# Down products of a split-precision FFN: eight PSUM banks in rotation instead of four

## What is computed

```python
def swiglu_ffn(x, g, w_gate, w_up, w_down):
    h = rmsnorm(x, g)
    return (jax.nn.silu(h @ w_gate) * (h @ w_up)) @ w_down

x = x + 0.5 * swiglu_ffn(x, ffn1_norm, ffn1_w_gate, ffn1_w_up, ffn1_w_down)
...                                    # mixers, cross attention
x = x + 0.5 * swiglu_ffn(x, ffn2_norm, ffn2_w_gate, ffn2_w_up, ffn2_w_down)
```

## Time and profile before

| | |
|---|---|
| runs shown | 3314.75, 3319.26, 3321.52 us; median 3319.26 |
| profiled execution, its own time | 3310.65 us |
| its span in the trace | 3308.9 us |
| TensorE matmul busy | 3157.0 us, 95% |
| VectorE busy | 1591.4 us, 48% |
| ScalarE busy | 925.1 us, 28% |
| GpSimd busy | 1164.7 us, 35% |
| mean granted TensorE clock | 0.991 of full speed |
| down phases of the 20 later turns: TensorE waits for `x_early`, `x_late` | 13.4 and 12.6 us |

### The profile page before, as it was taken

The page is one execution under the profiler, slowest core; times in us unless marked ns, Lnnn a source line. Parts: engine busy times, 40 slices in busy tenths (PEclk is TensorE's granted clock), DMA queues, the critical chain, the costliest instruction groups (busy, mean ns, idle before and its releaser), DMA issues.

```text
span 3308.9 us, 52314 instructions
## 1 busy us (share of the span) xinstructions
PE 3157.0 (95%) x19481; PEld 2993.7 (90%) x19481; DVE 1591.4 (48%) x2641; ACT 925.1 (28%) x1726; POOL 1164.7 (35%) x756
## 2 busy tenths in 40 slices
PE   6999999999999999999999999999899999999998
PEld 5999999999979888888887989988799999999997
DVE  3554445544546655653342456242328444455445
ACT  5222222212323333433423342132312222221123
POOL 3455555544422222211112034222124545444452
PEclk9999999999999999999999999999999999999999
DMA  5311111111143133211112145024301111111112
GB/s 186 134 39 39 51 38 57 45 38 38 66 149 130 56 130 124 82 62 49 65 43 75 49 160 177 28 91 168 132 32 39 39 45 44 38 58 43 38 38 77
DMA packets 92182, 247.52 MB, mean 75 GB/s; under 512 B 11536, under 2 KB 49168, under 8 KB 89360
## 3 DMA queue, kind: packets, MB, share of 16 engines
q1 hardware_dynamic: 48640, 154.09, 13.9%
q10 hardware_dynamic: 43408, 91.55, 7.7%
HBM read 197.87 MB, written 47.75 MB: 74 GB/s over the span
## 4 chain that ended last, share of the span: by engine, by line
PE 83%; DVE 9%; issue 3%; ACT 2%; POOL 1%; ACTq 1%; DVEq 0%; POOLq 0%
PE psum L168 55%; PE psum L264 13%; PE psum L2197 1%; DVE n_tmp L954 1%; PE psum L2133 1%; PE psum L1339 1%; PE psum L3167 1%; DVE f_h_hi L801 1%; PE psum L1409 1%; DVE f_hid L802 1%; PE psum L1384 1%; POOL w_lo L2672 1%; PE psum L3140 1%; DVE a_sc L1734 1%; PE psum L2147 1%
## 5 line engine op out<-in xcount | busy, mean ns | idle before, releaser
L133 POOL TENSOR_TENSOR w_hi<-w_raw,zero 128x1024 fp32r<-128x1024 f32 x79 | 158.9, 2012 | 1138.6 <-PE psum L264 788.7
L457 POOL TENSOR_TENSOR w_lo<-w_raw,w_hi 128x512 fp32r<-128x512 f32 x320 | 418.6, 1327 | 389.0 <-ACT w_hi L655 389.0
L168 PE MATMUL psum<-x_hi,w_hi 128*128 128x384 f32 x2288 | 463.8, 336 | 14.6 <-issue 4.6
L168 PE MATMUL psum<-x_lo,w_hi 128*128 128x384 f32 x2288 | 462.7, 336 | 0.0
L168 PE MATMUL psum<-x_hi,w_lo 128*128 128x384 f32 x2288 | 458.9, 334 | 0.0
L168 PEld LDWEIGHTS psum<-x_hi,w_hi 128*128 128x128 f32 x2288 | 402.1, 188 | 22.5 <-issue 13.2
L168 PEld LDWEIGHTS psum<-x_lo,w_hi 128*128 128x128 f32 x2288 | 404.2, 188 | 2.2 <-issue 0.6
L168 PEld LDWEIGHTS psum<-x_hi,w_lo 128*128 128x128 f32 x2288 | 402.2, 188 | 0.0
L168 PE MATMUL psum<-f_h_hi,w_hi 128*128 128x384 f32 x1056 | 271.8, 338 | 27.4 <-DVE x_early L760 13.4
L655 ACT ACTIVATE w_hi<-w_raw 128x512 fp32r<-128x512 f32 x320 | 192.6, 626 | 375.1 <-PE psum L168 312.2
L168 PE MATMUL psum<-f_h_hi,w_lo 128*128 128x384 f32 x1056 | 268.1, 334 | 0.0
(11 more groups left out here) (339 smaller groups left out, 4779.1 us busy)
## 6 DMA issues: line engine op xcount, KB each, us to landing
w_raw<-units SPq DMA_DIRECT2D x224, 512.0 KB, 3.8
gate_dram<-b_stash ACTq DMA_DIRECT2D x48, 192.0 KB, 1.9
e_gate<-gate_dram ACTq DMA_DIRECT2D x48, 192.0 KB, 2.7
a_kc<-k_cache ACTq DMA_DIRECT2D x4, 2048.0 KB, 8.5
a_vc<-v_cache ACTq DMA_DIRECT2D x4, 2048.0 KB, 13.0
proj_dram<-a_cv ACTq DMA_DIRECT2D x12, 576.0 KB, 2.8
b_pad<-proj_dram SPq DMA_DIRECT2D x12, 576.0 KB, 4.9
x_sk<-mem_k ACTq DMA_DIRECT2D x6, 1024.0 KB, 8.3
```

What stands on the lines that cost most here:

```text
L133: pool.tensor_tensor(k.w_hi[s][:, :], k.w_raw[s][:, :], k.zero[:, 0:1].to_broadcast([P, D]), ALU.add)\
L168: mm = pe.matmul(out, wl if part == 2 else wh, (xl if part == 1 else xh)[:, n0:n1], start=(part == 0 and i == 0), stop=(part == 2 and i == ...
L457: pool.tensor_tensor(half(k.w_lo, h), raw_of(p, name), half(k.w_hi, h).bitcast(F32), ALU.subtract)\
```

## The change

In turns 1 to 9 of both FFNs the down products rotate over all eight banks: down product j goes to bank j mod 8. Turns 0 and 10 stay at four. With that the waits move. Down products 0 to 3 wait as before. Down product 4 goes to bank 4 and waits for the fifth `f_h_hi` multiplication of the turn (`gate_used`), which was the last reader of that bank; down product 5 goes to bank 5 and waits for the turn's last pair sum (`c_added`); 6 and 7 have no wait of their own, and from 8 on down product j waits until j - 8 has been added. The first four jobs of `pair(i, 0)`, which use banks 4 to 7, now wait until down products 20 to 23 of the turn before have been added. VectorE's order is the same; it only reads from another bank.

```diff
+    def down_banks(i):
+
+        return NPS if isinstance(i, int) and i in (0, LAST) else 2 * NPS
...
             def bank_free(job):
                 if job >= 4:
                     bank_read(i, p, job - 4)
-                elif p:
+                elif not p:
+                    pe.wait_ge(k.x_added.sem, k.x_added.at(24 * i + (job + 1)))
+                else:
                     bank_read(i, 0, job + PAIR_JOBS - 4)
...
             g = 12
+            banks = down_banks(i)
             for n in range(3):
                 pe.wait_ge(k.h_ready.sem, k.h_ready.at(6 * i + ((4, 5, 6) if first else (4, 6, 6))[n]))
                 for d in range(KD):
                     if not first and n == 0 and d in (0, 4):
                         split(i, 2, "D1a" if d == 0 else "D1b")
-                    if not first or g >= 12 + NPS:
+                    if banks == 2 * NPS and NPS <= g - 12 < banks:
+                        if g == 12 + NPS:
+                            pe.wait_ge(k.gate_used.sem, k.gate_used.at(6 * i + 5 + 3))
+                        elif g == 13 + NPS:
+                            pe.wait_ge(k.c_added.sem, k.c_added.at(8 * i))
+                    elif banks == 2 * NPS and g >= 12 + banks:
+                        pe.wait_ge(k.x_added.sem, k.x_added.at(24 * i + (g - 12 - NPS + 1)))
+                    elif not first or g >= 12 + NPS:
                         pe.wait_ge(k.x_added.sem, k.x_added.at(24 * i + (g - 12 + 1)))
...
-                    mm = product(pe, k.ps[g % NPS][:, 0:THIRD], tiles, n * THIRD, (n + 1) * THIRD)
+                    mm = product(pe, k.ps[(g - 12) % banks][:, 0:THIRD], tiles, n * THIRD, (n + 1) * THIRD)
...
         def add_down(i, first):
             g = 12
+            banks = down_banks(i)
...
-                    dve.scalar_tensor_tensor(out=xs, in0=k.ps[g % NPS][:, 0:THIRD], scalar=0.5, in1=xs,
+                    dve.scalar_tensor_tensor(out=xs, in0=k.ps[(g - 12) % banks][:, 0:THIRD], scalar=0.5, in1=xs,
```

## The result

| | before | after |
|---|---|---|
| median of the runs | 3318.46 us (4 runs, 3314.75 to 3321.52) | 3288.36 us (4 runs, 3285.90 to 3290.04) |
| ratio, 95% interval | | 0.9909 (0.9892 to 0.9926) |
| span of the profiled execution | 3308.9 us | 3288.2 us |

The medians differ by 30.1 us, 24.6 to 35.8 by the interval; 27.2 were forecast, and a time of 3292 us in a range of 3283 to 3302. A second measurement of the changed kernel on another occasion gave 3289.19 against 3316.94 us, a ratio of 0.9917 (0.9902 to 0.9932), 27.8 us less.

The account below looks back on a forecast made before the run. TensorE, busy 95%, was taken as the bound, stalling once per turn at down product 4. Sixteen turns at 1.50 us (24.0) plus two at 1.58 (3.2) gave 27.2 us off the 3319.26 median: 3292 us, range 3283 to 3302.

Parts of the forecast that it names:

- The place of the loss: Turns 1 to 9 of each FFN: TensorE loses time only before down product 4, once per turn, waiting for VectorE's addition.
- The size of one wait: Down product 4: 1.50 us lost per turn, 1.39 waiting and 0.11 refilling; 1.58 us in turn 1.
- distance of starts: Pricing the stall at down product 4 by when matmuls start, since ends are modelled; gives 1.50 us per turn.
- idle figure of 1.22 us: TensorE's idle time shown before down product 4 in turn 2, first FFN; called too small because ends are modelled.
- refill of 0.11 us: Extra delay after TensorE's wait at down product 4, counted as 0.11 of the 1.50 us lost per turn.
- The waits behind it: Other waits from down product 4 on: cost nothing, with margins such as 4.0 us for `D1b` and 4.1 for down product 5.
- the waits of down product 8: Next possible stall: needs the last `f_h_lo` and addition 0; margins 3.3 and 2.8 us, so no cost.
- the head of the pair: Four new waits at jobs 0 to 3 of the next pair; taken as nothing, job 0 with 2.36 us to spare.
- upper bound of 7.9 us: Four new waits starting the next pair: one 0.11 us refill each, 0.44 us per turn, 7.9 us in all at most.
- The partial gain: Rival: pair start pays 7.9 us, or waiting for addition 23 costs 16.6 us; time 3300 or 3309; chance 0.07.
- "Nothing changes": Rival: another wait, `D1b`, ends last at down product 4, 5.3 us later than its row; time 3319, chance 0.02.
- the slower clock: Rival: down phases' matmuls run at 1.2 GHz, 25 us more per turn, 449 us in all; 3741 us, chance 0.02.

Follow-up runs that it names:

- Six banks: Against the changed kernel, down products of turns 1 to 9 rotate over six banks instead of eight; 3288.59 us, 0.9917 of the kernel before.
- five banks: Against the changed kernel, down products of turns 1 to 9 rotate over five banks instead of eight; 3303.91 us, 0.9951 of the kernel before.
- both kernels with four banks: Kernel before, with two GpSimd splits starting four down products later (3289.60 us, 0.9918), or additions 0 to 2 before the last hidden value's second multiplication (3282.56 us, 0.9900).
- late head: Against the changed kernel, job 0 of pair(i, 0) waits for addition 23 of the turn before instead of 20; 3309.37 us, 0.9975 of the kernel before.

## Why the prediction was right

**The place of the loss** was right: one wait per turn, at down product 4, for addition 0. Six banks, five banks and both kernels with four banks move or remove it as that says. What made VectorE late, the GpSimd splits, the prediction did not ask; it noted the 1.67 us of the multiplication without a reason.

**The size of one wait** was 1.50 us (1.58 in turn 1) by the distance of starts. The turns became 72.23 - 70.72 = 1.51 us shorter. The idle figure of 1.22 us would have given 22 us in place of 27; measured by the copies it is 27.4. The step from idle time to distance of starts mattered, and so did the refill of 0.11 us, which the five banks show by itself.

**The waits behind it** were worth nothing, as costed: `D1b`, `gate_used`, `c_added` and the waits of down product 8 never became the last. For the head of the pair I had kept an upper bound of 7.9 us from refills, 0.44 for each of 18 heads (with turn 10 there are 20, which makes 8.8). It is nothing; the late head shows what would be paid if the wait did bind.

**The rivals.** The partial gain used 0.92 us for a head that waits for addition 23, in 18 turns; measured in the kernel with the late head, it is 0.95, in 20. "Nothing changes" and the slower clock did not occur in the changed turns: their granted clock is 1.00. The page on the clock gate in the Trainium skill ("TensorE: Matmul & The Clock Gate", "A second HAM failure mode: psum-queue depth-cycling") blames pauses between groups, not the banks. The traces agree so far: rotating over eight banks left turns 1 to 9 at 1.00, and in the second FFN the lower clock was seen only behind the two pauses of turn 0, in four of the nine profiled executions that have them. That the pauses are its cause is likely and not shown.

**What was not foreseen** is that the profiled execution would give back 7 us in places which the change does not touch. The forecast for the median did not suffer, since the runs vary by as much. That the difference of medians in the first measurement, 30.1 us, is larger than the 27.4 us in the turns is likewise spread, and not a further gain of the change.

## What to carry to other kernels

When one engine waits for another to free a buffer, ask first why the other is late: here the same 1.5 us per turn could be had with four more banks, with two more banks, by moving two GpSimd operations four products later, or by putting three instructions of VectorE ahead of one. More buffers are the cover, and one too few leaves a remainder that can be worked out from the rows. Price a stall by the distance of starts against an undisturbed stretch, and then look for what is due next behind the same instruction, with its margin.

## What the runs showed of the hardware

- VectorE's `tensor_tensor` with all operands in SBUF took 1.67 and 1.64 us instead of 0.56 while GpSimd ran its own on SBUF, and up to 2.73 us in turn 10. In the four places of the kernel before where both ends can be read, it ended 0.41 or 0.42 us after the GpSimd instruction beside it. Additions that read one operand from PSUM kept 0.49 us in a row beside GpSimd (1.47 us for three).
- After pauses of 1.42 and 1.47 us, whose ends lie 2.8 us apart, TensorE ran for about 3.6 us at 0.32 us per matmul of 384 columns instead of 0.1733. It did so in four of nine profiled executions with these pauses (in the changed kernel granted clock 0.92 over 22 us, 100 matmuls) and not in the other five (in the kernel before 1.00, 109 matmuls). In the kernel before, single pauses of 1.2 us once per turn left the clock at 1.00.
- A wait that is met before it is reached cost nothing on TensorE that the starts show (turns of 70.72 us for 408 matmuls of 0.1733), with a register instruction ahead of it or without.
